# Scores of a forgetting attention over 128 rows, with one selector matmul for both parts of the cumulated gates

## The reference

```python
def forgetting_attention(q, k, v, f_logit):        # 16 heads of 64
    cum = jnp.cumsum(jax.nn.log_sigmoid(f_logit.astype(jnp.float32)), axis=1).transpose(0, 2, 1)
    scale = 1.0 / math.sqrt(HEAD_DIM)
    for blk in range(s // Q_BLOCK):                # two blocks of 128 queries
        qs, qe = blk * Q_BLOCK, (blk + 1) * Q_BLOCK
        sc = jnp.einsum("bhqd,bhkd->bhqk", q[:, :, qs:qe], k[:, :, :qe]).astype(jnp.float32) * scale
        sc = sc + cum[:, :, qs:qe, None] - cum[:, :, None, :qe]
        allowed = jnp.arange(qe)[None, :] <= jnp.arange(qs, qe)[:, None]
        sc = jnp.where(allowed, sc, -jnp.inf)
        p = jax.nn.softmax(sc, axis=-1).astype(v.dtype)
        outs.append(jnp.einsum("bhqk,bhkd->bhqd", p, v[:, :, :qe]))
```

## Time and profile before

| | us |
|---|---|
| median of three runs | 1228.63 |
| the profiled execution | 1229.91 |
| its span, first to last instruction | 1228.1 |
| TensorE busy | 1202.7 (98%) |
| VectorE busy | 855.8 (70%) |
| ScalarE busy | 681.4 (55%) |
| GpSimd busy | 372.3 (30%) |
| granted clock of TensorE, mean | 0.993 |

### The profile page before, as it was taken

The page is one execution under the profiler, slowest core; times in us unless marked ns, Lnnn a source line. Parts: engine busy times, 40 slices in busy tenths (PEclk is TensorE's granted clock), DMA queues, the critical chain, the costliest instruction groups (busy, mean ns, idle before and its releaser), DMA issues.

```text
span 1228.1 us, 26084 instructions
## 1 busy us (share of the span) xinstructions
PE 1202.7 (98%) x9746; PEld 1177.4 (96%) x9746; DVE 855.8 (70%) x1221; ACT 681.4 (55%) x1019; POOL 372.3 (30%) x402
## 2 busy tenths in 40 slices
PE   8999999999999999998999989999999999999996
PEld 8999888999989999998999989999999999999996
DVE  7877666787699999547898586555566768555553
ACT  6597544654566776445754546555445546555442
POOL 3244000430345555212000155444220007444321
PEclk9999999999999999999999999999999999999998
DMA  6567322466626555662634245656765536566662
GB/s 223 174 191 210 114 90 90 131 211 213 227 87 186 179 182 186 208 177 86 187 119 132 76 145 181 187 175 185 259 203 166 169 113 185 183 183 186 191 203 69
DMA packets 56567, 204.52 MB, mean 167 GB/s; under 512 B 6640, under 2 KB 6776, under 8 KB 56368
## 3 DMA queue, kind: packets, MB, share of 16 engines
q1 hardware_dynamic: 54288, 197.35, 52.5%
q0 software_dynamic: 1632, 5.11, 1.2%
q10 hardware_dynamic: 576, 1.05, 0.2%
HBM read 202.43 MB, written 2.63 MB: 167 GB/s over the span
## 4 chain that ended last, share of the span: by engine, by line
PE 91%; DVE 6%; ACT 1%; DMA 1%; POOL 0%; issue 0%; SPq 0%; DVEq 0%; ACTq 0%
PE bank L1320 26%; PE bank L1321 25%; PE bank L1322 25%; PE bank L1579 2%; PE bank L1413 2%; PE bank L1414 2%; PE bank L1415 2%; PE bank L1502 1%; DVE w_lo L656 1%; DVE h_lo L686 1%; DVE work L811 1%; DMA raw<-in_stream 1%; PE bank L1504 1%; DVE work L710 1%; PE bank L1491 1%; DVE work L677 1%
## 5 line engine op out<-in xcount | busy, mean ns | idle before, releaser
L656 DVE TENSOR_TENSOR w_lo<-raw,w_hi 128x1024 fp32r<-128x1024 f32 x374 | 488.0, 1313 | 151.1 <-ACT w_hi L268 147.7
L1320 PE MATMUL bank<-h_hi,w_hi 128*128 128x256 f32 x1888 | 542.6, 287 | 11.1 <-DVE h_lo L686 6.4
L1321 PE MATMUL bank<-h_lo,w_hi 128*128 128x256 f32 x1888 | 535.7, 284 | 0.0
L1322 PE MATMUL bank<-h_hi,w_lo 128*128 128x256 f32 x1888 | 535.6, 284 | 0.0
L268 ACT ACTIVATE w_hi<-raw 128x1024 fp32r<-128x1024 f32 x374 | 391.9, 1052 | 200.7 <-PE bank L1322 190.0
L1320 PEld LDWEIGHTS bank<-h_hi,w_hi 128*128 128x128 f32 x1888 | 363.5, 193 | 17.8 <-issue 7.6
L1321 PEld LDWEIGHTS bank<-h_lo,w_hi 128*128 128x128 f32 x1888 | 363.8, 193 | 0.3
L1322 PEld LDWEIGHTS bank<-h_hi,w_lo 128*128 128x128 f32 x1888 | 363.5, 193 | 0.0
L1320 PE MATMUL bank<-u_hi,w_hi 128*128 128x256 f32 x868 | 247.5, 285 | 3.1 <-DVE u_lo L1065 2.0
L1321 PE MATMUL bank<-u_lo,w_hi 128*128 128x256 f32 x868 | 246.2, 284 | 0.0
L1322 PE MATMUL bank<-u_hi,w_lo 128*128 128x256 f32 x868 | 246.1, 284 | 0.0
(11 more groups left out here) (228 smaller groups left out, 1219.3 us busy)
## 6 DMA issues: line engine op xcount, KB each, us to landing
raw<-in_stream SPq DMA_DIRECT2D x374, 512.0 KB, 3.7
bias_rows<-bias_row POOLq DMA_DIRECT2D x1, 1536.0 KB, 15.7
work<-in_x_t SPq DMA_DIRECT2D x2, 512.0 KB, 6.2
work<-in_x_t POOLq DMA_DIRECT2D x1, 1024.0 KB, 6.4
work<-bias_rows POOLq DMA_DIRECT2D x1, 1024.0 KB, 12.7
out<-work ACTq DMA_DIRECT2D x4, 256.0 KB, 2.5
work<-in_lmask POOLq DMA_DIRECT2D x1, 512.0 KB, 8.2
work<-bias_rows POOLq DMA_DIRECT2D x1, 512.0 KB, 8.3
```

What stands on the lines that cost most here:

```text
L656: v.tensor_tensor(w_lo[:, slot, :], raw[:, slot, :], w_hi[:, slot, :].bitcast(F32), ALU.subtract).then_inc(lo_ready, 1)
L1320: mm(out, w_hi[:, slot, s], r_hi, start=start, stop=False)
L1321: mm(out, w_hi[:, slot, s], r_lo, start=False, stop=False)
L1322: return mm(out, w_lo[:, slot, s], r_hi, start=False, stop=stop)
```

## The change

The queries get two areas, one with the first head of each pair in rows 0 to 63 and zeroes below, one with the second head in rows 64 to 127 and zeroes above (units 20 to 27 and 52 to 59). GpSimd zeroes both once X has been split, in the place where the split of the gates stood. VectorE evacuates each query tile in two halves of 64 rows, one into each area. High and low part of the cumulated gates lie in one unit, `CUM_TWO`, on partitions 0 to 15 and 32 to 47, with zeroes elsewhere, and the selector has an identity at both places. So a head's scores are, for each query block, one f32 matmul over 128 rows and one fp32r matmul over 128 rows. The split and the two copies of the identity move from GpSimd to VectorE, into step 2 of the phase `ga`, before that step's `lru_gain`. GpSimd zeroes `CUM_TWO` and `EYE_R` at its start. TensorE waits on three semaphores before `qk` in place of one.

```diff
--- before.py
+++ after.py
@@ -117,11 +117,12 @@
         table = F[0:BUCKETS, 46, 0:H_MOBA]
 
         XA, GA, XC = F[:, 0:10, :], F[:, 0:10, :], F[:, 10:20, :]
-        Q, K, V = F[:, 20:28, :], F[:, 28:36, :], F[:, 36:44, :]
+        QZ = [F[:, 20:28, :], F[:, 52:60, :]]
+        K, V = F[:, 28:36, :], F[:, 36:44, :]
         WF_HI, WF_LO = (u[:, 2 * R + 2, 0:C * H_FOX] for u in (u_hi, u_lo))
 
-        CUM_HI, CUM_LO = u_hi[0:H_FOX, 2 * R, :], u_lo[0:H_FOX, 2 * R, :]
-        EYE_R = u_hi[0:H_FOX, 2 * R + 1, 0:H_FOX]
+        CUM_TWO, EYE_R = u_hi[:, 2 * R, :], u_hi[:, 2 * R + 1, 0:H_FOX]
+        CUM_HI, CUM_LO = u_hi[0:H_FOX, 2 * R, :], u_hi[32:32 + H_FOX, 2 * R, :]
         SGA, SGB = F[:, 44:52, :], F[:, 52:60, :]
         RG, IG, ASQ = F[:, 60:70, :], F[:, 70:80, :], F[:, 48:50, :]
         PRA, PRB = F[:, 70:78, :], F[:, 0:8, :]
@@ -169,8 +170,9 @@
         ext_mm, ext_ready = sem("bias_rows_made"), sem("bias_rows_ready")
         act_step, dve_step, pool_step = sem("act_step"), sem("dve_step"), sem("pool_step")
         der_ready, sp_ln, lb_exp = sem("derived_ready"), sem("softplus_ln"), sem("lb_exp")
-        f_mm, f_ln, cum_ready, cumt_mm, cumt_ready, cum_split = (
-            sem(n) for n in ("f_mm", "f_ln", "cum_ready", "cum_t_mm", "cum_t_ready", "cum_split"))
+        f_mm, f_ln, cum_ready, cumt_mm, cumt_ready, cum_split, cum_zero, cum_eye, qz_zero = (
+            sem(n) for n in ("f_mm", "f_ln", "cum_ready", "cum_t_mm", "cum_t_ready", "cum_split", "cum_zeroed", "head_rows",
+                             "queries_zeroed"))
         tap_done, taps_done, xch_ready, xcl_ready = (
             sem(n) for n in ("tap_done", "taps_done", "xc_hi_ready", "xc_lo_ready"))
         gates_evac, ix_done, tanh_done, decay_done, gain_done, root_done, scan_done, ya_done, yah, yal = (
@@ -851,9 +853,20 @@
                     v.scalar_tensor_tensor(out=att_s[:, b, a:e], in0=bank[4 + b][:, a:e], scalar=cum_t[:, j, n:n + 1],
                                            in1=mask[:, a:e], op0=ALU.add, op1=ALU.add).then_inc(s_evac, 1)
 
+            def forget_split():
+                dve.wait_ge(cum_zero, 2)
+                dve.wait_ge(cum_ready, 1)
+                v.tensor_copy(CUM_HI, ncum[:, :]).then_inc(cum_split, 1)
+                dve.wait_ge(cum_split, 1)
+                v.tensor_tensor(CUM_LO, ncum[:, :], CUM_HI.bitcast(F32), ALU.subtract).then_inc(cum_split, 1)
+                for o in (0, 32):
+                    v.tensor_copy(EYE_R[o:o + H_FOX, :], ident[o:o + H_FOX, o:o + H_FOX]).then_inc(cum_eye, 1)
+
             dve.wait_ge(cst_in, 32)
             for t in range(R):
                 step("ga", t)
+                if t == 2:
+                    forget_split()
                 if t >= 1:
                     lru_gain(t - 1)
                 if t == 4:
@@ -879,8 +892,12 @@
                 elif s % 2:
                     normed(K[:, t, :], TILE["qk"] + s)
                 else:
-                    v.scalar_tensor_tensor(out=Q[:, t, :], in0=out_of(TILE["qk"] + s), scalar=DH_FOX ** -0.5, in1=RSTD,
-                                           op0=ALU.mult, op1=ALU.mult).then_inc(evacuated, 1)
+                    for o in (0, DH_FOX):
+                        rows = slice(o, o + DH_FOX)
+                        ins = v.scalar_tensor_tensor(out=QZ[o // DH_FOX][rows, t, :], in0=out_of(TILE["qk"] + s)[rows, :],
+                                                     scalar=DH_FOX ** -0.5, in1=RSTD[rows, :], op0=ALU.mult,
+                                                     op1=ALU.mult)
+                    ins.then_inc(evacuated, 1)
                 if s == 0:
                     lru_gain(R - 1)
                 if 0 <= s - 2 < H_FOX:
@@ -1188,6 +1205,8 @@
             pool.dma_start(ident[:, :], ident_d).then_inc(cst_in, 16)
             pool.dma_start(mask[:, :], mask_d).then_inc(cst_in, 16)
             g.memset(ONES_ROW, 1.0).then_inc(one_row, 1)
+            g.memset(CUM_TWO.bitcast(F32), 0.0).then_inc(cum_zero, 1)
+            g.memset(EYE_R.bitcast(F32), 0.0).then_inc(cum_zero, 1)
             pair_sums("mix")
 
             for t in range(R):
@@ -1198,12 +1217,10 @@
 
             pool.dma_start(bass.AP(tensor=row, offset=0, ap=[[EXT, H_MOBA], [1, EXT]]), ext).then_inc(row_out, 16)
 
-            pool.wait_ge(cst_in, 32)
-            g.tensor_copy(EYE_R, ident[0:H_FOX, 0:H_FOX]).then_inc(cum_split, 1)
-            pool.wait_ge(cum_ready, 1)
-            g.tensor_copy(CUM_HI, ncum[:, :]).then_inc(cum_split, 1)
-            pool.wait_ge(cum_split, 2)
-            g.tensor_tensor(CUM_LO, ncum[:, :], CUM_HI.bitcast(F32), ALU.subtract).then_inc(cum_split, 1)
+            pool.wait_ge(hh_ready, C)
+            pool.wait_ge(hl_ready, C)
+            for q in QZ:
+                g.memset(q, 0.0).then_inc(qz_zero, 1)
 
             for t in range(R):
                 pool.wait_ge(gates_evac, t + 1)
@@ -1493,16 +1510,14 @@
 
             def fox_scores(h):
 
-                t, o, out = h // 2, h % 2 * DH_FOX, bank[4 + h % 2]
+                t, out = h // 2, bank[4 + h % 2]
                 pe.wait_ge(evacuated, TILE["qk"] + 2 * t + 2)
                 if h >= 2:
                     pe.wait_ge(s_evac, 2 * h - 2)
-                sel = EYE_R[:, h:h + 1].to_broadcast([H_FOX, P])
+                sel = EYE_R[:, h:h + 1].to_broadcast([P, P])
                 for a, e, qb in ((0, P, 0), (P, EXT, 1)):
-                    mm(out[:, a:e], Q[o:o + DH_FOX, t, qb * P:(qb + 1) * P], K[o:o + DH_FOX, t, 0:e - a],
-                       start=True, stop=False)
-                    mm(out[:, a:e], sel, CUM_HI[:, 0:e - a], start=False, stop=False)
-                    last = mm(out[:, a:e], sel, CUM_LO[:, 0:e - a], start=False, stop=True)
+                    mm(out[:, a:e], QZ[h % 2][:, t, qb * P:(qb + 1) * P], K[:, t, 0:e - a], start=True, stop=False)
+                    last = mm(out[:, a:e], sel, CUM_TWO[:, 0:e - a], start=False, stop=True)
                 last.then_inc(s_mm, 1)
 
             def values(n, out, vt):
@@ -1523,7 +1538,9 @@
 
             pe.wait_ge(gates_evac, 2 * R)
             pe.wait_ge(cumt_ready, 1)
-            pe.wait_ge(cum_split, 3)
+            pe.wait_ge(cum_split, 2)
+            pe.wait_ge(cum_eye, 2)
+            pe.wait_ge(qz_zero, 2)
             for s in range(3 * C):
                 tile(0, PART["qk"] + s, TILE["qk"] + s)
                 if 0 <= s - 4 < H_FOX:
```

## The result

The changed kernel takes 1212.98 us (median of four runs, 1211.44 to 1214.62) against 1228.69 us; the ratio is 0.9873, 95% interval 0.9862 to 0.9885. That is 15.7 us less, where 1213 us and 15.5 were forecast. The profiled execution took 1212.74 us, its span 1210.9. That the median falls within 0.1 us of the forecast is luck: the four executions lie up to 3.2 us apart, and the changed kernel measured once more in another comparison took 1214.13 us, 14.5 less than the kernel before.

The account below looks back on a forecast made before the run. TensorE was taken to bound the kernel, with 91% of the chain. 13 x 0.94 + 3 x 1.11 = 15.5 us saved, all else costing nothing, took 1228.63 to 1213.1, rounded to 1213; range 1209.5 to 1219.

Parts of the forecast that it names:

- The scores: Forgetting attention: each head's scores fall from 1.83 to 0.89 us; sixteen heads save 15.5 us.
- two full-row selectors: New scores of each head: selector matmuls over 128 rows cost 0.11 us for 128 columns and 0.12 for 256.
- VectorE's halves: Query tiles evacuated in two halves: eight times one more VectorE instruction of 0.42 us, costing nothing.
- the 0.71 us of stall: Old scores of each head: 1.12 us of work in 1.83; the other 0.71 stands at changes of row count.
- five changes: Old scores of each head: from 128 rows to 64, 16, 64, 16 and out again, together 0.71 us.
- No loading ahead: Rival for the new scores: full-row weights wait for the matmul before, scores cost 1.55 us, time 1223.6; chance 0.02.
- Mixed types: Rival for the scores: stalls come from mixing f32 and fp32r and remain; gain 6.4 us, time 1222.2; chance 0.06.
- VectorE's chain: Rival in the heads: VectorE sets part of the step, held at about 5.5 us; time 1219.8; chance 0.06.
- VectorE's cover: In the heads, two evacuations end about 4.70 us after a shift, the next due at 5.08: fits by 0.38.
- an overrun would stop nobody: In the heads: a VectorE shift late by less than a step stops nobody, as TensorE has a step in hand.
- The split and the zeroes: Gate branch: split adds 1.0 us on VectorE, 2.0 if GpSimd slows it; two GpSimd fills, 1.83 each; cost nothing.
- The clock: Half-speed dip around 344 to 348 us may fall away or be added when shifted; worth at most 1.7 us.

Follow-up runs that it names:

- the next improvement: The changed kernel with a head's values over all 128 output rows of its pair, in place of 64 columns: 1209.99 us, ratio 0.9844 to the kernel before.

## Why the prediction was right

**The scores.** 0.89 us were forecast for the new scores and 5.08 for the step; the trace has 5.08, and 15.6 us from the gate branch to the first norm against a sum of 15.5. The estimate for two full-row selectors, 0.23, was borne out from the other side by 0.22 for two more. VectorE's halves, the split and the zeroes cost TensorE nothing, as forecast. The sum came out because each of its terms stood in a row of this kernel: the other attention had already priced f32 scores over 128 rows, and a stream of short matmuls the weight load.

**The cause.** The forecast put the 0.71 us of stall to the changes of the row count on the ground that the other attention had none. The runs show it, and with the borders counted as above one price fits all of them:

| | changes counted | us | us each |
|---|---|---|---|
| before, step | 4 | 0.71 | 0.18 |
| before, head without values | 5 | 1.99 - 1.12 = 0.87 | 0.17 |
| selector over 64 rows, step | 3 | 0.52 | 0.17 |
| the same, head without values | 4 | 0.71 | 0.18 |
| all over 64 rows, step | 1 | 0.20 | 0.20 |
| the same, head without values | 2 | 0.39 | 0.20 |
| before without selectors, step | 1 | 0.20 | 0.20 |
| the same, head without values | 2 | 0.37 | 0.19 |
| values over 128 columns | 2 | 0.32 | 0.16 |

The forecast listed five changes for the 0.71 us, though by its own remark the way into the values is in the 4.19 us already. Its sum doesn't suffer, because it took 1.83 us as a whole; the first expectations do, which took 0.14 each and so 0.57 for what are three changes of 0.17, and 0.28 for one of 0.20. That 0.57 came near 0.52 is two errors that cancel. Why a change costs this much no run shows.

**The rivals.** "No loading ahead" is out: three transposes over the same 128 rows follow each other at 0.11 us, and the new scores cost 0.89 us and not 1.55. The Trainium skill's rule for it (TensorE: Matmul & The Clock Gate, "Part 3: Packing small matmuls — row/col tiling") disagrees with this trace in this use, where full matmuls follow each other at 0.12 us. The rule of the Trainium skill that may bear on the case is in TensorEngine Tiling (Array Packing), section "Tiling Modes": changing the tiling mode drains TensorE. It gives no price, and no trace here shows a mode; if a matmul over fewer rows or columns is such a change, the runs agree, with 0.16 to 0.20 us for each. Mixed types are out by the run with the selector over 64 rows and by the one over 64 rows throughout. VectorE's chain is out as a bound of the heads: the changed kernel has no wait of TensorE in them.

**VectorE's cover.** The extra half was forecast to end 0.38 us ahead of the next shift. VectorE's timeline of the kernel after, two shifts, one behind an even and one behind an odd step:

```profile
174.82 0.74 DVE L853 SCALAR_TENSOR_TENSOR att_s<-bank,cum_t,mask 128x128 f32<-128x128 f32 x2 [0.36 <-PE bank L1520]
...
179.89 0.74 DVE L853 SCALAR_TENSOR_TENSOR att_s<-bank,cum_t,mask 128x128 f32<-128x128 f32 x2 [0.79 <-PE bank L1520]
```

The wait in front of the shift is 0.36 where two halves were evacuated and 0.79 where one tile was, against 1.74 before. That an overrun would stop nobody was argued then. For an overrun of 0.55 us it holds in all steps but one, where TensorE lost 0.8 us.

**The split and the zeroes.** Four small instructions were put at 1.0 us, 2.0 beside GpSimd. VectorE's timeline in the gate branch:

```profile
97.69 0.69 DVE L859 CAST u_hi<-ncum 16x256 fp32r<-16x256 f32 x1
98.41 0.85 DVE L861 TENSOR_TENSOR u_hi<-ncum,u_hi 16x256 fp32r<-16x256 f32 x1
99.29 0.36 DVE L863 CAST u_hi<-ident 16x16 fp32r<-16x16 f32 x2
...
101.92 1.76 DVE L658 TENSOR_TENSOR w_lo<-raw,w_hi 128x1024 fp32r<-128x1024 f32 x1
```

They take 0.69, 0.85 and 0.36 for two, 1.9 in all: the forecast's upper bound was the value. GpSimd works beside the first two; that this makes them slow is not shown. The low half for tile 6 starts at 101.92, against 101.97 before, and takes 1.76 us in place of 1.23; TensorE's tiles don't wait for it: the ten of the gate branch take 117.60 - 88.72 = 28.9 us, as before. The two fills took 3.58 us on GpSimd, 3.66 were counted, and lie in its idle time.

**The clock.** It stood in the forecast as up to 1.7 us either way and was 1.5 us in the profiled pair. From line 1627's first start to line 1357's the kernel before takes 923.6 - 691.2 = 232.4 us, with the granted clock low in two places; the changed kernel takes 230.9 in both of its profiled executions, with one such place; with the split on GpSimd it is 229.4, with none. So the steps of 1.5 us are dips. The one of the earlier trace rows did not fall away: the changed kernel has it too, 15.7 us earlier (1.97 us idle ahead of 328.36, then 0.77 from 330 to 335). The one that did is near 730 us before. Whether the changed kernel has one less there as a rule, the two executions don't settle; the first medians don't need it, 15.7 us against 15.6 from the heads, but they are not exact to 1 us.

**What the forecast had wrong** is in its readings, not in its sum. It said that the first product over 128 rows would show 0.23 us from start to start; it shows 0.14, though the step is as forecast, so such a start-to-start time is no price. And it said 0.89 us from the first product to the values' first matmul, which is 0.98, for the way into 64 columns stands there as well. Its count of five changes is set right above.

## What to carry to other kernels

A small matmul that uses fewer rows or columns of the array than its neighbours costs 0.16 to 0.20 us at each border, more than its own work of 0.11 in this kernel; pad it with zeroes to the neighbours' shape, or at least give all small ones between two large blocks the same shape. Price such a block by the length of the whole step, with and without it, and look for the same work in another shape elsewhere in the same trace. Before a stage on one engine is made shorter, look at which engine has a fixed block of work right behind it: 1.6 of the 5.1 us of the next improvement were given back there. And when counting borders, leave out those that stand there with and without the block.

## What was not expected of the hardware

A change of the column count alone costs as well: the values over 64 columns, between full matmuls, cost 0.32 us more per head than over 128 (5.08 against 4.76), with the same number of columns streamed. A price of 0.16 to 0.20 us is the same, within what the traces tell, between 128 and 64 rows, between 64 and 16, and between 128 and 64 columns. A two-part evacuation of 64 rows each costs twice one of 128 rows on ScalarE and VectorE, 0.77 and 0.85 us for two against 0.39 and 0.41 for one.
